# Decoder block on one core: compression products moved ahead of half 8, and the program's end issued in other pieces

## The reference

```python
h = rms_norm(x, ln_attn_pre)
proj = h @ w_in                                   # queries, keys, values, gates
kc = silu(blocks_of(k_cmp) @ w1 + b1) @ w2        # nsa_compress: 63 blocks of 32 tokens x 64,
vc = silu(blocks_of(v_cmp) @ w1 + b1) @ w2        #   2048 -> 256 -> 64
mix = concat[nsa(q, kc, vc, ...), sliding_window(...), stick_breaking(...)], each rms_norm-ed
x = x + rms_norm(mix @ w_out, ln_attn_post)
h = rms_norm(x, ln_ffn_pre)
f = (silu(h @ w_gate) * (h @ w_up)) @ w_down      # 2816 wide
x = x + rms_norm(f, ln_ffn_post)
```

## Time and profile before

| | us |
|---|---|
| median of 3 runs | 1290.91 |
| lowest and highest | 1289.54 and 1294.75 |
| profiled execution, its own time | 1290.52 |
| its span | 1288.5 |
| PE busy | 1249.8 (97%) |
| DVE busy | 868.1 (67%) |
| ACT busy | 602.1 (47%) |
| POOL busy | 245.8 (19%) |

### The profile page before, as it was taken

How to read it: one execution, slowest core, us unless ns; L and a number is a source line. 1 busy time by engine, 2 the same in 40 slices (tenths; PEclk the granted TensorE clock), 3 DMA queues, 4 the chain that set the end, 5 groups by cost and what they waited for, 6 DMA issues and landing times.

```text
span 1288.5 us, 19180 instructions
## 1 busy us (share of the span) xinstructions
PE 1249.8 (97%) x6776; PEld 1072.8 (83%) x6776; DVE 868.1 (67%) x1607; ACT 602.1 (47%) x1139; POOL 245.8 (19%) x194
## 2 busy tenths in 40 slices
PE   7999899999999999999999999999999999999998
PEld 6898678889989899888878888888888887788887
DVE  4322698858868756356786666557656659969875
ACT  5432577657757545434553333333333436544441
POOL 4230111111000000011001122112112137607112
PEclk9999899999989999999999999999999999999998
DMA  6303412136842000222402332333232367373433
GB/s 227 116 2 99 115 50 50 33 96 159 181 124 79 18 18 1 60 91 97 146 21 88 123 113 68 106 123 122 84 122 80 128 209 261 109 229 88 139 132 131
DMA packets 66882, 136.44 MB, mean 106 GB/s; under 512 B 8631, under 2 KB 27327, under 8 KB 66788
## 3 DMA queue, kind: packets, MB, share of 16 engines
q1 hardware_dynamic: 66788, 135.22, 34.1%
HBM read 89.81 MB, written 28.60 MB: 92 GB/s over the span
## 4 chain that ended last, share of the span: by engine, by line
PE 82%; DVE 9%; issue 4%; ACT 3%; POOL 1%; DMA 1%; DVEq 0%; SPq 0%; ACTq 0%; POOLq 0%
PE ps L2350 31%; PE ps L2380 13%; PE ps L1013 7%; PE ps L2294 6%; PE ps L991 4%; PE ps L884 4%; PE ps L865 4%; PE ps L824 4%; PE ps L956 2%; PE ps L964 2%; DVE ring L1383 2%; DVE ring L1375 1%; DVE f_headL L2186 1%; DVE m_rows_sb L1390 1%; DVE f_W L2147 1%
## 5 line engine op out<-in xcount | busy, mean ns | idle before, releaser
L2350 PE MATMUL ps<-f_topH,f_W 128*128 128x512 f32 x704 | 220.7, 389 | 0.7 <-ACT QT L1952 0.7
L2350 PEld LDWEIGHTS ps<-f_topH,f_W 128*128 128x128 f32 x704 | 132.2, 188 | 28.4 <-DVE f_W L2147 1.1
L2350 PE MATMUL ps<-f_topL,f_W 128*128 128x512 f32 x352 | 136.9, 389 | 0.0
L1013 PE MATMUL ps<-V,m_tw 128*128 128x66 f32 (+1 forms) x1056 | 129.9, 273 | 1.1 <-DVE m_mix_n L1427 1.1
L2380 PE MATMUL ps<-f_headH,f_W 128*128 128x512 f32 x408 | 128.5, 390 | 1.2 <-DVE QT L2181 1.1
L1013 PEld LDWEIGHTS ps<-V,m_tw 128*128 128x128 f32 x1056 | 127.3, 193 | 2.4 <-DVE m_mix_n L1427 1.5
L2350 PE MATMUL ps<-f_headH,f_W 128*128 128x512 f32 x352 | 114.9, 390 | 2.4 <-DVE f_p1a L2154 2.4
L2147 DVE TENSOR_TENSOR f_W<-f_scr,f_W 128x512 fp32r<-128x512 f32 x88 | 62.0, 708 | 78.7 <-ACT f_W L1939 78.6
L2147 DVE TENSOR_TENSOR f_W<-ring,f_W 128x512 fp32r<-128x512 f32 (+1 forms) x84 | 77.3, 929 | 42.8 <-ACT f_W L1939 42.8
L2380 PEld LDWEIGHTS ps<-f_headH,f_W 128*128 128x128 f32 x408 | 76.6, 188 | 18.0 <-issue 2.0
L1193 ACT COPY m_tw<-ps 128x512 f32<-128x512 f32 (+4 forms) x93 | 52.9, 583 | 67.0 <-PE ps L991 36.4
(11 more groups left out here) (279 smaller groups left out, 2921.9 us busy)
## 6 DMA issues: line engine op xcount, KB each, us to landing
act_pairs<-QT SPq DMA_DIRECT2D x77, 256.0 KB, 4.2
f_stage<-act_pairs SPq DMA_DIRECT2D x77, 256.0 KB, 2.7
m_qs<-m_qn SPq DMA_DIRECT2D x128, 128.0 KB, 2.4
ring<-in_ffn_w_up SPq DMA_DIRECT2D x22, 512.0 KB, 3.7
ring<-in_ffn_w_gate SPq DMA_DIRECT2D x19, 512.0 KB, 4.9
ring<-in_w_in_tiles SPq DMA_DIRECT2D x9, 512.0 KB, 3.6
ring<-in_nsa_phi_w SPq DMA_DIRECT2D x8, 512.0 KB, 5.1
ring<-in_w_out SPq DMA_DIRECT2D x8, 512.0 KB, 5.6
```

The lines of the kernel that those rows point to most:

```text
L1013: ins = pe.matmul(ps[:, SUMS, wide * i:wide * (i + 1)], tw[0:w, t % W_SLOTS, P * i:P * i + P], v, start=(kb == 0 and i == 0), stop=(kb == ...
L2350: ins = pe.matmul(ps[:, bank, :], whole[:, w, cols], halves[h][:, k0 + k, col:col + HALF], start=(begins and k == 0 and w == 0 and h == 0) ...
```

## The change

It has four parts.

1. PE issues `phi_hidden(0..7)` ahead of the pieces of half 8, and the first of them waits for `tab_copied` 2 (before, that wait stood in the first piece). On ScalarE the exponential stands ahead of `half_keep(8)` and `cut_hi(10)`; on VectorE `cut_lo(10)` stands behind SiLU's last multiplication.
2. The first half of `x`'s first block, the gain and the first half of the first weights count on one semaphore, `first_in`, and who waited for one of them waits for all three (48). The separate wait for the gain goes.
3. The last product's add on VectorE is made in two adds of 256 columns. The square of tile 7 (h = 1), the sum over it, the mean and the root are made in two parts of two token tiles each, in two banks. For h = 1 POOL also adds the square of tile 6, so that the early moment has half the matmuls. `apply_gain` of tile 7 stands ahead of `early_mean`.
4. PE turns the first six feature tiles of token tile 4 ahead of the moments and the last two behind them; a turn waits for the gains tile by tile. Token tiles 6 and 7 are finished in halves: the left 512 columns by VectorE, the right ones scaled by ScalarE from `ps` and added to the residual by POOL, with a store of 256 KB for each half.

```diff
@@ pe_program of mixers
             def phi_hidden(c):
                 i = c // 4
+                if c == 0:
+                    pe.wait_ge(tab_copied, 2)
                 wait_loaded(pe, "phi", c)
...
             values(NT - 1)
+            for c in range(NPHI):
+                phi_hidden(c)
             for s in range(EARLY_PIECE, FIRST_PIECE):
                 piece(s)
-            for c in range(NPHI):
-                phi_hidden(c)
             pe.wait_ge(silu_step, 4)
@@ act_program of mixers
-                        act.wait_ge(x_in[0] if hf else first_x_in, 16)
+                        act.wait_ge(x_in[0] if hf else first_in, 16 if hf else 16 * 3)
...
-                    act.wait_ge(first_w_in, 16)
+                    act.wait_ge(first_in, 16 * 3)
...
-            act.wait_ge(gain_in, 16)
...
+            act.wait_ge(silu_step, 1)
+            act.activation(sig[:], hid[:], ACT.Exp, scale=-1.0).then_inc(e_done, 1)
             half_keep(EARLY)
             cut_hi(FIRST_ITEMS - 1)
-            act.wait_ge(silu_step, 1)
-            act.activation(sig[:], hid[:], ACT.Exp, scale=-1.0).then_inc(e_done, 1)
@@ dve_program of mixers
-            dve.wait_ge(gain_in, 16)
+            dve.wait_ge(first_in, 16 * 3)
...
-            cut_lo(FIRST_ITEMS - 1)
             dve.wait_ge(tab_out, 32)
...
             dve.tensor_tensor(hid[:], hid[:], sig[:], ALU.mult).then_inc(silu_step, 1)
+            cut_lo(FIRST_ITEMS - 1)
@@ sp_program of out_and_ffn
-        for t in range(NT):
+        for t in range(6):
             fin.store(sp, t)
-        sp.wait_ge(fin.out_done, 16 * NT)
+        for t in range(6, NT):
+            fin.store_halves(sp, t)
+        sp.wait_ge(fin.out_done, 16 * (NT + 2))
@@ pool_program
-            for m in range(1, KT - 2):
+            for m in range(1, KT - 2 + h):
                 fin.add_square(pool, h, m)
...
-        fin.root(pool, 1)
+        for a in range(2):
+            fin.last_root(pool, a)
+        for t in (6, 7):
+            fin.add_half(pool, t)
@@ act_program
-                wait_taken(act, kind, u, m)
-                fin.square(act, h, i)
+                if (h, i) == (1, KT - 1):
+                    for a in range(2):
+                        act.wait_ge(y_added, added_at[kind, u, m] + 1 + a)
+                        fin.last_square(act, a)
+                else:
+                    wait_taken(act, kind, u, m)
+                    fin.square(act, h, i)
+        for t in (6, 7):
+            fin.scale_half(act, t)
@@ dve_program, add_out and the end
-            dve.tensor_tensor(part, ps[:, down_bank(kind, m), :], part, ALU.add).then_inc(y_added, 1)
+            if s < NS - 1:
+                dve.tensor_tensor(part, product_, part, ALU.add).then_inc(y_added, 1)
+            else:
+                for cols in (slice(0, HALF // 2), slice(HALF // 2, HALF)):
+                    dve.tensor_tensor(part[:, cols], product_[:, cols], part[:, cols], ALU.add).then_inc(y_added, 1)
...
+        fin.apply_gain(dve, 1, KT - 1)
         fin.early_mean(dve, 1)
-        fin.apply_gain(dve, 1, KT - 1)
-        fin.mean(dve, 1)
-        for t in range(4, NT):
+        for a in range(2):
+            fin.last_mean(dve, a)
+        for t in range(4, 6):
             fin.norm(dve, t)
+        for t in range(6, NT):
+            fin.norm_half(dve, t)
@@ pe_program, the end
+        fin.turn(pe, 4, range(0, KT - 2))
+        wait_taken(pe, "D3", LAST_ROUND, M_PAIRS - 2)
         fin.early_moment(pe, 1)
-        wait_taken(pe, "D3", LAST_ROUND, M_PAIRS - 1)
-        fin.late_moment(pe, 1)
-        for t in range(4, NT):
+        pe.wait_ge(y_added, added_at["D3", LAST_ROUND, M_PAIRS - 1] + 2)
+        for a in range(2):
+            fin.last_moment(pe, a)
+        fin.turn(pe, 4, range(KT - 2, KT))
+        for t in range(5, NT):
             fin.turn(pe, t)
@@ class Finish, new
+    def last_moment(self, pe, a):
+        pe.wait_ge(self.squares, 2 * KT + a)
+        for q in (2 * a, 2 * a + 1):
+            ins = pe.matmul(self.ps[:, LATE_BANKS[a], q:q + 1], self.sq[1][:, 1, q * P:(q + 1) * P], self.ones[:], start=True, stop=True)
+        ins.then_inc(self.moments, 1)
+
+    def last_root(self, pool, a):
+        cols = slice(4 + 2 * a, 6 + 2 * a)
+        pool.wait_ge(self.ms_done, 4 + a)
+        pool.tensor_tensor(self.rs[:, cols], self.ms[:, cols], self.mhalf[:, 0:2], ALU.pow).then_inc(self.rs_done, 1)
+
+    def scale_half(self, act, t):
+        act.wait_ge(self.y_turned, t + 1)
+        act.wait_ge(self.rs_done, 3)
+        act.activation(self.sq[1][:, t % 2, :], self.ps[:, self.bank(t) + 1, :], ACT.Copy,
+                       scale=self.rs[:, t:t + 1]).then_inc(self.half_scaled, 1)
+
+    def add_half(self, pool, t):
+        part = self.room(t)[:, HALF:D]
+        pool.wait_ge(self.half_scaled, t - 5)
+        pool.wait_ge(self.x_in[t % 4], 32)
+        pool.tensor_tensor(part, self.sq[1][:, t % 2, :], part, ALU.add).then_inc(self.half_added, 1)
...
+    def store_halves(self, sp, t):
+        sp.wait_ge(self.sum_done, t + 1)
+        sp.dma_start(self.out[t * P:(t + 1) * P, 0:HALF], self.room(t)[:, 0:HALF]).then_inc(self.out_done, 16)
+        sp.wait_ge(self.half_added, t - 5)
+        sp.dma_start(self.out[t * P:(t + 1) * P, HALF:D], self.room(t)[:, HALF:D]).then_inc(self.out_done, 16)
...
-        if t == 1 or t == 7:
-            pe.wait_ge(self.ms_done, 2 * (t // 4) + 2)
+        if t in (1, 6, 7):
+            pe.wait_ge(self.ms_done, 2 if t == 1 else 5)
```

More of the change, by code:

```diff
@@ L2266, in dve_program @@
                 if kind == "D5" and m < 2:
-                    (fin.early_mean, fin.mean)[m](dve, 0)
+                    fin.mean(dve) if m else fin.early_mean(dve, 0)
                 n = s - place["D5", LAST_ROUND, 0]
@@ L2474, in apply_gain @@
         dve.wait_ge(self.g_in, 16)
-        dve.wait_ge(self.squares, KT * h + m + 1)
+        dve.wait_ge(self.squares, KT * h + m + 1 + (h == 1 and m == KT - 1))
         dve.tensor_scalar(part, part, self.gain[:, n:n + 1], None, ALU.mult).then_inc(self.gained, 1)
@@ L2490, in early_moment @@
         pe.wait_ge(self.mhalf_set, 2)
-        pe.wait_ge(self.acc_done, 5 * h + 5)
+        pe.wait_ge(self.acc_done, 6 * h + 5)
         pe.wait_ge(self.squares, KT * h + KT - 1)
+        sums = ((self.acc[:, h, :], True),) if h else ((self.acc[:, h, :], True), (self.sq[h][:, 0, :], False))
         for q in range(4):
-            for rows, first in ((self.acc[:, h, :], True), (self.sq[h][:, 0, :], False)):
+            for rows, first in sums:
                 ins = pe.matmul(self.ps[:, self.moment_bank(h), 4 + q:5 + q], rows[:, q * P:(q + 1) * P], self.ones[:],
-                                start=first, stop=not first)
+                                start=first, stop=h == 1 or not first)
@@ L2504, in late_moment, with last_square @@
                             start=True, stop=True)
         ins.then_inc(self.moments, 1)
+    def last_square(self, act, a):
+        if a == 0:
+            act.wait_ge(self.acc_done, 10)
+        cols = slice(a * HALF // 2, (a + 1) * HALF // 2)
+        n = self.tile(1, KT - 1)
+        act.activation(self.sq[1][:, 1, cols], self.yT[:, n, HALF:][:, cols], ACT.Square).then_inc(self.squares, 1)
+    def last_moment(self, pe, a):
[3 more added lines that the diff above has]
+        ins.then_inc(self.moments, 1)
@@ new lines, in last_mean @@
+    def last_mean(self, dve, a):
+        part = self.ms[:, 4 + 2 * a:6 + 2 * a]
+        dve.wait_ge(self.moments, 4 + a)
+        dve.wait_ge(self.ms_done, 3)
+        dve.scalar_tensor_tensor(out=part, in0=self.ps[:, LATE_BANKS[a], 2 * a:2 * a + 2], scalar=1.0 / D,
+                                 in1=part, op0=ALU.mult, op1=ALU.add).then_inc(self.ms_done, 1)
+    def last_root(self, pool, a):
+        cols = slice(4 + 2 * a, 6 + 2 * a)
+        pool.wait_ge(self.ms_done, 4 + a)
+        pool.tensor_tensor(self.rs[:, cols], self.ms[:, cols], self.mhalf[:, 0:2], ALU.pow).then_inc(self.rs_done, 1)
@@ new lines, in norm_half @@
+    def norm_half(self, dve, t):
+        part = self.room(t)[:, 0:HALF]
+        dve.wait_ge(self.y_turned, t + 1)
+        dve.wait_ge(self.rs_done, 3)
+        dve.wait_ge(self.x_in[t % 4], 32)
+        dve.scalar_tensor_tensor(out=part, in0=self.ps[:, self.bank(t), :], scalar=self.rs[:, t:t + 1], in1=part,
+                                 op0=ALU.mult, op1=ALU.add).then_inc(self.sum_done, 1)
+    def store_halves(self, sp, t):
[3 more added lines that the diff above has]
+        sp.dma_start(self.out[t * P:(t + 1) * P, HALF:D], self.room(t)[:, HALF:D]).then_inc(self.out_done, 16)
@@ L2510, in early_mean, with mean, root, turn @@
                           ALU.mult, ALU.add).then_inc(self.ms_done, 1)
-    def mean(self, dve, h):
-        dve.wait_ge(self.moments, 2 * h + 2)
-        dve.wait_ge(self.ms_done, 2 * h + 1)
-        dve.scalar_tensor_tensor(out=self.ms[:, 4 * h:4 * h + 4], in0=self.ps[:, self.moment_bank(h), 0:4], scalar=1.0 / D,
```

(28 more changed lines are left out.)

26 lines of the change are left out of this document (14 added, 12 removed).

## The result

| | kernel before | changed kernel |
|---|---|---|
| median, us | 1292.2 (1289.5 to 1294.8, 4 runs) | 1283.04 (1280.9 to 1284.6, 4 runs) |
| ratio, 95% interval | | 0.9932 [0.9907, 0.9957] |
| profiled execution: time, span, us | 1290.52, 1288.5 | 1284.56, 1282.6 |
| last product's end to the span's end (R to end), us | 14.43 | 11.78 |

The change wins 9.2 us between the medians, of 10.6 forecast by the sum's terms (7.6 + 0 + 3.0). The time, 1283.0, is inside the whole range and 0.5 above the forecast's own range. It was timed again beside two of the experiments' sets, with ratios of 0.9935 [0.9918, 0.9951] and 0.9926 [0.9907, 0.9945].

A forecast was written before the change was run, and what follows sets the result against it. PE (TensorE), busy 97% of the span, bounds the kernel; only its standstill or half-clock time can be won. 1290.5 − 7.6 (compression order) − 0 (semaphore) − 3.0 (end) = 1279.9 us; own range 1277.5 to 1282.5, whole range 1275.5 to 1286.5.

The forecast's parts named there:

- PE's standstill: PE waits for SiLU after the compression products, 129.7 to 135.25 us; the new order was to remove these 5.5 us.
- The clock from 130 to 140: PE's granted clock after the compression was to be 1.00 from 130 to 140 us; it was 0.53 after the standstill.
- The lead at the first scores, 7.6: PE was to reach the first attention scores at 137.25 us instead of 144.84, 7.6 us earlier.
- The queries, 0.25 us of spare: The first query group was to be ready at 137.0 us, 0.25 us before PE wants it for the first scores.
- The first rival: Queries 1.4 us late hold the first scores; 4.65 us won there for 7.6, time 1282.8 us; chance 0.10.
- POOL beside VectorE: Port-lock rule: POOL's query scaling delays VectorE's cuts, first scores at 137.4, term 7.5, sum 1280.0; left out of the sum.
- Part 2, 0: Merging the first loads' semaphore at the start was to cost 0, or 0.6 us if its cover is gone.
- Part 3, 3.0: New end after the last product: 3.0 us won, between 4.2 at full clock and 1.9 at lower; bounds 0.3 and 4.5.
- 256 KB take 2.0, and 0.4 of span follows: At the end, the last half store was to take 2.0 us, with 0.4 us more to the span's end.
- The attention stage gives it back: Rival: the attention stage loses the earlier gain, only the end is won, 1287.5 us; chance 0.12.
- the prediction's own sign: Distance from first scores to last product was to stay 1129.2 us; longer would show the attention stage giving time back.
- The clock from 376 to 400, slower or quicker: Rivals: shifted work gets clock 0.72, costing 17 us, 1297, chance 0.04; or low stretches vanish, 1275.9, chance 0.06.

The follow-up runs named there:

- e10_queries: Changed kernel with the second query copies ahead of tile 7's load and VectorE's cut of item 10 behind its first two query remainders: 1281.80 us, ratio 0.9927.
- e9_best: Changed kernel with e10_queries' two edits and token tiles 4 and 5 normed and stored in halves: 1281.86 us.
- a_third: The changed kernel itself, timed a third time beside other experiments: 1281.75 us.
- a_again: The changed kernel itself, timed again beside its parts: 1282.06 us, against 1290.54 of the kernel before.
- e6_spread_first: Changed kernel with the second group of query copies queued ahead of tile 7's load: 1282.55 us, ratio 0.9934.
- e8_halves: Changed kernel with token tiles 4 and 5 normed and stored in halves: 1283.58 us.
- e1_order: Kernel before with only compression ahead of half 8 and SiLU ahead of item 10's cuts: 1283.53 us, ratio 0.9947.
- e3_first: Kernel before with only the merged semaphore for the first three loads: 1291.43 us, ratio 1.0005.
- e2_end: Changed kernel without the new order of compression and SiLU; merged semaphore and new end stay: 1289.59 us, ratio 0.9990.
- e4_cuts_only: Kernel before with only SiLU ahead of item 10's cuts on ScalarE and VectorE, PE's order kept: 1289.3 us, ratio 0.9991.
- e5_phi_only: Kernel before with only PE's compression products ahead of half 8, the cuts left in place: 1291.79 us, ratio 1.0011.

## Why the prediction was right, point by point

- **PE's standstill.** Right. Forecast: no idle time before the end products, 5.5 us won. There is none.
- **The clock from 130 to 140.** Right: 1.00 and 5.54 us for half 8.
- **The lead at the first scores, 7.6.** Measured 7.45 to 7.60 where the queries are late, and 7.92 in e10_queries and e9_best, where they aren't.
- **The queries, 0.25 us of spare.** Mis-sized: they came late, with 0.15 to 0.17 us of idle time on PE, worth 0.33 from start to start. The stage ran 1.2 us later than forecast as a whole (start), so the issue at 134.10 is the 132.9 of the forecast; from it to the first scores it took 4.5 us for 4.1. The first rival, 1.4 us late, did not happen. What the sum left out is the *second* group: its copies stand behind tile 7's load. They held PE for 0.40 us in the changed kernel, 0.27 in a_third and not at all in a_again, and from the first scores to 158.8 us these three lost 0.8, 0.7 and 0.4 us of lead, e6_spread_first 0.1.
- **POOL beside VectorE.** The rule beats the sum here. DVE's cut of 128x512 took 1.38 us beside POOL's scaling (131.53 to 132.83):

```profile
131.53 1.30 POOL L804 TENSOR_TENSOR QT<-QT 128x512 f32<-128x512 f32 x1 [52.39 <-ACT QT L1096]
```
```profile
131.99 1.38 DVE L1266 TENSOR_TENSOR m_wL<-ring,m_wH 128x512 fp32r<-128x512 f32 x1 [2.75 <-ACT m_wH L1080]
135.11 0.69 DVE L1266 TENSOR_TENSOR m_wL<-ring,m_wH 128x512 fp32r<-128x512 f32 x1 [0.71 <-ACT m_wH L1080]
```

  The same cut without POOL beside it took 0.69, and the slow one ended 0.54 after POOL. By the Trainium skill, "SBUF — State Buffer" (SBUF: two separate sides), the pair of ports is an exclusive lock between the two engines; the trace agrees, within 0.15 us (0.69 behind POOL's end would be 133.52, the cut ended at 133.37). The price on the path was paid too: with the start taken out the first scores are at 137.4, which is what I had worked out beside the sum (a term of 7.5), and e10_queries, with the cut moved away, has them 0.33 earlier. The sum was near all the same because a wait that it lacked and a stage 0.3 us quicker than it said nearly cancel (7.92 − 0.33 for 7.6). That part is luck.
- **Part 2, 0.** Right within the measurement (1.0005).
- **Part 3, 3.0.** This is the term that was mis-sized: 1.5 to 1.8 in the medians. Up to the last add every step came out: R + 7.6 for + 7.75, clock 1.00. The step that failed is "256 KB take 2.0, and 0.4 of span follows", 2.4 us; it took 4.1. The 0.4 held, in all 14 profiles. The 2.0 holds for a half with nothing ahead of it (2.0 in e8_halves). But the last half is issued 0.24 after the add, and takes 3.5, because others are still moving. I had priced the store alone, by a row of stores that were issued 1.2 to 1.7 us apart and moved nearly alone. With the norms in halves on three engines, 2 MB come ready within 3.4 us (tile 4's norm to the last add) and need 5.1 at 406 GB/s. By the Trainium skill, "DMA: Bandwidth & Descriptors" (Anatomy of one DMA), 2.0 us fixed and the bytes at 436 GB/s, a half store would take 2.6, an estimate. The page gives that for DMAs issued by GpSimd; here SyncE issues them, and no run bears it out: 2.0 for the half and 2.6 for the whole.
- **Where luck came in.** At full clock the end was to win 4.2 us, and it won 2.6 in the profiles. The 3.0 of the sum is nearer to what was measured because it is the middle between full and lower clock, and the lower clock didn't come. It is no better worked out for it.
- **What the old end costs.** Rows 10 to 12 showed one execution, 14.4 us. In e1_order the clock fell later and the same end took 13.0, in e3_first 14.3; the new one took 11.8 in all six profiles that have it unchanged. By the profiles the new end is worth 1.1 to 2.6, by where the clock falls in the old one.
- **The attention stage gives it back.** Not shown as an effect of the change, nor wholly excluded. The changed kernel's lead falls from 6.9 to 4.5 over the stage, but a_third keeps 7.1. By the prediction's own sign, the distance from the first scores to the last product (1129.2 before), the three profiles of the changed kernel have 1132.2, 1133.0 and 1129.7, and e2_end and e3_first, with PE's old order, 1131.7 and 1130.0: before was the shortest of its kind. The losses in the profiles are the wait at 304 us, which kernels with the old order have too, and a stretch at the lower clock at 457.6 that e2_end has as well (from about 465), and a_third and e1_order lack. Over all profiles the distance is 1131.1 on average with all of part 1 and 1130.4 without; 0.7 us may be given back, and the spread (1127.6 to 1133.0) doesn't tell it from none.
- **The clock from 376 to 400, slower or quicker.** Neither came. It averaged 0.79 for 0.72, and between 0.66 and 0.93 over all profiles, 0.79 in e4_cuts_only with the old order.

In sum, 7.0 + 0 + 1.5 to 1.8 is 8.5 to 8.8, and 8.5, 9.2 and 9.3 were measured for the whole (the first 8.5 is the same by its making, since the 1.5 is counted to a_again). Of the 3.1 us between 1279.9 and 1283.0, 1.7 are the reference: the sum started from 1290.5, and the kernel before had 1292.2 as its median beside the changed kernel. The other 1.4 are the parts, 9.2 for 10.6.

## What to carry to other kernels

When a product is moved ahead to cover a chain on other engines, move what stands in front of that chain on those engines too: each half of this move was worth about nothing alone, both 7.0 us. Price a store by what is still moving when it is issued: the price of a store with nothing ahead of it (2.0 us here) is too low for the last of several that come ready together (3.5). And before a loss late in one trace is put down to the change, look for the same wait in traces that lack the change.

## What the runs showed of the hardware

- A vector operation of 0.69 us took 1.38 beside a GpSimd operation of 1.30 (1.22 in e5_phi_only) and ended about 0.5 us behind it. On the path to the first scores this cost 0.33 us.
- PE's clock fell to its lower level while PE stood still (4.0 and 6.3 us in e4_cuts_only and e5_phi_only), whether narrow or wide matmuls had run before, and it did not fall in the changed kernel, where 128 products of 63 columns ran on into wide ones. It fell at other times with PE busy (104 to 107 us in e3_first). With the old end it fell at different points of equal programs (R to end 13.0 and 14.4).
- Stores on SyncE's queue, from issue to landing: 2.0 us for 256 KB with nothing ahead (2.4 in one trace), 2.6 for 512 KB, 3.5 for the last 256 KB of 2 MB that move together at 406 GB/s. From the last landing to the end of the span 0.4 us passed in every profile.
